# First mixer of a two-block network on one core: state space and attention interleaved pair by pair with 33 projection chunks

## The chip, the cores and the metric

The kernel runs on one core of a Trainium2 chip. The metric is device time in microseconds (us) of one execution of the whole program; lower is better. TensorE (PE) multiplies, VectorE (DVE) and ScalarE (ACT) do the elementwise work, GpSimd (POOL) does a few small things, and SyncE (SP) issues every DMA. Each engine runs its own list of instructions strictly in order and waits on semaphores for the others.

## The reference

The network has two blocks over 256 tokens of width 1024, all in float32. The change touches only the mixer of the first block, and none of its mathematics:

```python
def hybrid_mixer(h, ...):
    z, xbc, dt_raw, q, k, v, g_ssd, g_att = split_columns(h @ w_in)
    y_ssd = ssd_mixer(z, xbc, dt_raw, ...) @ w_ssd_out
    q, k = rope(q, positions), rope(k, positions)
    y_att = moba_attention(q, k, v) @ w_attn_out      # one block of 256 keys: causal softmax
    merged = sigmoid(g_ssd) * y_ssd + sigmoid(g_att) * y_att
    return merged @ w_out

def ssd_mixer(z, xbc, dt_raw, ...):                   # 16 heads of 64, 2 groups, state 64
    xs, Bm, Cm = split(silu(causal_dwconv(xbc, conv_w, conv_b)))
    dt = softplus(dt_raw + dt_bias); A_cum = cumsum(-dt * exp(a_log))
    y = (C B^T masked, times exp(A_cum[l] - A_cum[s])) @ (xs * dt) + xs * d_skip
    yg = (y * silu(z)) in 2 groups of 512 columns
    return yg * rsqrt(mean(yg * yg, last axis) + 1e-6) * norm_w
```

After the mixer come a mixture of experts, a gated embedding and a second block of four layers. They are the same in both kernels.

## The kernel before

**Chunks.** Every large weight is streamed in chunks of 1 MB (1024 rows by 256 columns) through three slots (`RING` = 3). SP loads chunk c into `raw` when chunk c-3's low part has been made. ACT copies it to `ring_hi`, rounded to fp32r (function `high`, called by `part`, L1716), when PE has used chunk c-3; DVE takes the rest into `ring_lo` (`low`, L2163). PE multiplies a chunk in 48 products of 256 columns, high by high, high by low and low by high (`product_f` L904, `product_t` L923), and DVE reads the result from PSUM ("drains" it; `drain`, L2187). `chunk_used` and `drained` count the chunks that PE has finished and that DVE has read.

**Stages.** The mixer runs as a sequence of stages: 9 + 8 + 4 + 8 chunks of the input projection (`in_zx`, `in_qk`, `in_v`, `in_g`), then the state space (`ssd`, a loop over pairs of heads, two pairs a round), 4 chunks of `ssd_out`, then attention (`attention`, the same kind of loop), 4 chunks of `attn_out`, `ple`, and 4 chunks of `mix_out`. No chunk is multiplied while `ssd` or `attention` runs. What sets the order on each engine is the order in which the code calls its pieces.

**One pair of heads in `ssd`.** PE spreads the summed decays over the partitions (L1020), DVE takes gaps from them (L2344), ACT takes exp (L1855), DVE weighs them with C B^T (L2351), PE multiplies with the weighted inputs (L1029, L1031), DVE adds the skip (L2357) and the gate (L2360). After the eight pairs, the norm of each group g of 512 columns goes: ACT squares (L1861), PE sums the squares over partitions and so leaves the sum in every partition (L1038), ACT takes the square root with scale and eps (L1865, which loads a table), DVE takes the reciprocal (L2365), multiplies (L2368) and splits into high and low parts (L2373, L2374) for `ssd_out`.

**One pair of heads in `attention`.** PE rotates q and k with a matrix (L1048), DVE combines with cosine and sine (L2418 to L2423), PE scores (L1058), DVE masks and takes the row maximum (L2388, L2393), ACT takes exp (L1771), DVE divides by the sum (L2401), PE transposes (L1075), ACT and DVE copy the halves (L1775, L2406), PE multiplies by the values (L1085, L1087), ACT and DVE split the result (L1778, L2410).

**POOL** computes 1/sqrt for the token norms as a power of -0.5 (`norm_root`, L1672, two columns) and, in the second block, powers of 16 columns (L1692), a product of 256 columns (L1675) and sums of 768 columns (L1703).

Of the kernel before, what the change touches and what calls it, by code (L numbers as in the profile page):

```python
# [26 lines left out]
P = 128  # L27
SEQ, D = 256, 1024
# [23 lines left out]
CREDIT = 1  # L52
# [4 lines left out]
STREAM = [("in_zx", 9), ("in_qk", 8), ("in_v", 4), ("in_g", 8), ("ssd_out", 4), ("attn_out", 4), ("ple", 1), ("mix_out", 4),  # L57
# [28 lines left out]
H_READY = [o for o in OPERANDS if o not in ("na", "hyena")]  # L86
# [230 lines left out]
def build(nc, A, out):  # L317
# [5 lines left out]
    with ctx:  # L323
# [48 lines left out]
        cum_diag = at("cum_diag", [HEADS, HEADS, SEQ], 71 * KB)  # L372
# [29 lines left out]
        sq_buf = at("sq_buf", [P, 4, SEQ], 71 * KB)  # L402
        ynorm = at("ynorm", [P, 4, SEQ], 75 * KB)
        rstd = at("rstd", [P, SEQ], 79 * KB)

        rope_t = at("rope_t", [P, 2, SEQ], 58 * KB)
        rope_u = at("rope_u", [P, 2, SEQ], 60 * KB)

        qk_st = [at(f"qk_st{u}", [P, 2, SEQ], (62, 87)[u] * KB) for u in range(2)]
        v_st = [at(f"v_st{u}", [P, TT, 2 * HD], (64, 89)[u] * KB) for u in range(2)]  # L410

        probs = [at(f"probs{u}", [P, 2, TT * SEQ], (65, 78)[u] * KB) for u in range(2)]
        probs_t = [at(f"probs_t{u}", [P, 2, TT * SEQ], (69, 82)[u] * KB) for u in range(2)]
        at_max = [at(f"at_max{u}", [P, 2, TT], 73 * KB + 96 * u) for u in range(2)]
        at_sum = [at(f"at_sum{u}", [P, 2, TT], 73 * KB + 96 * u + 32) for u in range(2)]
        at_inv = [at(f"at_inv{u}", [P, 2, TT], 73 * KB + 96 * u + 64) for u in range(2)]
# [89 lines left out]
        p_t = at("p_t", [P, TT, SEQ], 8 * KB)  # L506
        p_hi = at("p_hi", [P, 2, SEQ], 10 * KB, f32r)
        p_lo = at("p_lo", [P, 2, SEQ], 12 * KB, f32r)
# [43 lines left out]
        scores = [acc[:, 0:2, :], acc[:, 2:4, :]]  # L552
        turned_p = [[proj[:, 0, :], proj[:, 1, :]], [proj[:, 2, :], misc[:, :]]]
# [5 lines left out]
        def pair_of(bank):  # L559
# [34 lines left out]
        v_staged, p_turned, pt_act, pt_dve, o_ready, o_hi, o_read = (  # L594
            sem("v_staged"), sem("p_turned"), sem("pt_act"), sem("pt_dve"), sem("o_ready"), sem("o_hi"), sem("o_read"))
# [23 lines left out]
        xdt_ready, y_gated = sem("xdt_ready"), sem("y_gated")  # L619
# [33 lines left out]
        def unsorted_bank(q):  # L653

            return proj[:, q, :] if q < RING else misc[:, :]

# [41 lines left out]
        def _(sp):  # L698
# [84 lines left out]
            load_cols("in_zx", A["w_in"][0], 0, {0: load_params})  # L783
            for dst, src in ((tri[:, :, :], A["tri"].rearrange("p (t n) -> p t n", t=TT)), (diag16[:, :], A["diag16"]),
                             (dt_bias[:, :], A["dt_bias"][0].partition_broadcast(P)),
                             (a_log_b[:, :], A["a_log"][0].partition_broadcast(P)),
                             (w_dt[:, :, :], A["w_in"][0].rearrange("(k p) n -> p k n", p=P)[:, :, DT_COL:DT_COL + HEADS]),
                             (d_col[0:HD, :], A["d_skip"][0].rearrange("(i a) -> a i", a=2)[0].partition_broadcast(HD)),
                             (d_col[HD:P, :], A["d_skip"][0].rearrange("(i a) -> a i", a=2)[1].partition_broadcast(HD)),
                             (inv_freq[:, :], A["inv_freq"]), (rot[:, :], A["rot"]), (causal[:, :], A["causal"]),  # L790
                             (pos_i[:, :], A["positions"][0].partition_broadcast(P))):
                sp.dma_start(dst, src, allow_slow_non_contiguous=True).then_inc(mixer_tables, 16)
# [90 lines left out]
        def _(pe):  # L883
# [2220 lines left out]
```

## Time and profile before

| | us |
|---|---|
| median of 3 runs (2139.34 to 2152.94) | 2142.66 |
| the profiled execution's own time | 2141.7 |
| its span from the first to the last instruction | 2139.9 |
| mixer's first product to its last `attn_out` product | 19.89 to 384.7 |
| PE busy, share of the span | 93% |
| DVE busy | 65% |
| ACT busy | 43% |

The profiled execution is 0.96 us below the median. In the page's second part (40 slices of 53.5 us), PE stands at 9 tenths nearly everywhere, and falls to 5 to 8 tenths in slices 5 to 9, which are the mixer. In the same slices the row of the granted TensorE clock falls to 5 to 9 tenths, and the DMA row to nearly nothing in two of them.

### The profile page before, as it was taken

To read this page: it belongs to the slowest core of one execution; us is meant where nothing else is said; L and a number is where in the kernel's file an instruction comes from. 1 tells how busy PE (TensorE), PEld (TensorE's weight loads), DVE (VectorE), ACT (ScalarE), POOL (GpSimd) and SP (SyncE) were. 2 spreads that over 40 slices of the span, in tenths; PEclk is the share of its full clock that TensorE was granted. 3 is DMA by queue.
4 is the path that set the end of the run, shared out by engine and by line. 5 is a ranking of instruction groups with operands and counts; after the bars stand their busy time and mean duration, and the time that the engine had idled before them with its cause. 6 is when DMAs were issued, how large, how long until landed. Compare 5 with 4: busy or idle time off the path is not lost.

```text
span 2139.9 us, 33097 instructions
## 1 busy us (share of the span) xinstructions
PE 1982.1 (93%) x13478; PEld 1805.0 (84%) x13478; DVE 1396.8 (65%) x1579; ACT 917.5 (43%) x980; POOL 46.3 (2%) x65
## 2 busy tenths in 40 slices
PE   7999577889999997999999999998997999999999
PEld 6998365867777776999998999997887999999998
DVE  4566766576767766576666755557998555675665
ACT  4344233365656655343334543333434333434332
POOL 0000000000000000000101100000000000000000
PEclk9999587989999999999999999999999999999999
DMA  6644030167777774745554337554224555554553
GB/s 207 204 139 157 0 104 8 58 244 289 294 273 270 289 266 150 211 139 187 199 188 154 117 126 241 180 178 137 92 67 138 174 180 177 176 177 148 195 189 117
DMA packets 243909, 365.94 MB, mean 171 GB/s; under 512 B 12566, under 2 KB 217961, under 8 KB 231401
## 3 DMA queue, kind: packets, MB, share of 16 engines
q1 hardware_dynamic: 243817, 364.64, 50.4%
q8 instruction: 67, 1.10, 0.2%
q14 instruction: 25, 0.20, 0.0%
HBM read 363.57 MB, written 1.05 MB: 170 GB/s over the span
## 4 chain that ended last, share of the span: by engine, by line
PE 57%; DVE 12%; DMA 5%; ACT 4%; issue 3%; DVEq 0%; POOL 0%; ACTq 0%
PE proj L904 30%; PE acc L1098 10%; PE proj L923 7%; DMA raw<-in_w_exp_up_dram 5%; PE proj L1281 3%; DVE ring_lo L2163 2%; DVE ring_lo L2620 2%; PE acc L1251 2%; ACT ring_hi L1890 1%; ACT second_hi L1890 1%; ACT ring_hi L1716 1%; DVE second_lo L2620 1%; PE acc L1111 1%; PE acc L1357 1%; PE acc L948 1%
## 5 line engine op out<-in xcount | busy, mean ns | idle before, releaser
L2163 DVE TENSOR_TENSOR ring_lo<-raw,ring_hi 128x2048 fp32r<-128x2048 f32 x242 | 560.7, 2318 | 258.1 <-ACT ring_hi L1716 257.6
L1716 ACT ACTIVATE ring_hi<-raw 128x2048 fp32r<-128x2048 f32 x242 | 462.2, 1912 | 540.0 <-PE proj L904 300.3
L904 PE MATMUL proj<-h_hi,ring_hi 128*128 128x256 f32 x1936 | 558.3, 288 | 21.6 <-DVEq L2199 9.5
L904 PE MATMUL proj<-h_lo,ring_hi 128*128 128x256 f32 x1936 | 550.0, 284 | 0.0
L904 PE MATMUL proj<-h_hi,ring_lo 128*128 128x256 f32 x1936 | 549.9, 284 | 0.0
L904 PEld LDWEIGHTS proj<-h_hi,ring_hi 128*128 128x128 f32 x1936 | 372.9, 193 | 32.5 <-issue 21.8
L904 PEld LDWEIGHTS proj<-h_lo,ring_hi 128*128 128x128 f32 x1936 | 372.9, 193 | 2.5 <-issue 1.4
L904 PEld LDWEIGHTS proj<-h_hi,ring_lo 128*128 128x128 f32 x1936 | 372.6, 192 | 0.0
L904 PE MATMUL proj<-g_hi,ring_hi 128*128 128x256 f32 x704 | 196.4, 279 | 4.1 <-DVE hid L2470 4.1
L904 PE MATMUL proj<-g_lo,ring_hi 128*128 128x256 f32 x704 | 195.7, 278 | 0.0
L904 PE MATMUL proj<-g_hi,ring_lo 128*128 128x256 f32 x704 | 195.6, 278 | 0.0
L904 PEld LDWEIGHTS proj<-g_hi,ring_hi 128*128 128x128 f32 x704 | 133.0, 189 | 5.3 <-issue 4.5
L904 PEld LDWEIGHTS proj<-g_lo,ring_hi 128*128 128x128 f32 x704 | 133.2, 189 | 0.8
L904 PEld LDWEIGHTS proj<-g_hi,ring_lo 128*128 128x128 f32 x704 | 133.0, 189 | 0.0
L2620 DVE TENSOR_TENSOR second_lo<-raw,second_hi 128x2048 fp32r<-128x2048 f32 x48 | 109.9, 2292 | 32.4 <-ACT second_hi L1890 32.2
L2620 DVE TENSOR_TENSOR ring_lo<-raw,ring_hi 128x2048 fp32r<-128x2048 f32 x48 | 109.3, 2290 | 24.6 <-ACT ring_hi L1890 24.6
L1790 ACT ACTIVATE silu_g<-gate_in 128x512 f32<-128x512 f32 x44 | 27.8, 632 | 198.2 <-DVE gate_in L2461 198.2
L1890 ACT ACTIVATE second_hi<-raw 128x2048 fp32r<-128x2048 f32 x48 | 92.0, 1917 | 35.2 <-DMA raw<-in_w_exp_up_dram 16.9
L923 PE MATMUL proj<-ring_hi,h_hi 128*128 128x256 f32 x320 | 94.9, 297 | 9.2 <-DVE h_lo L2528 8.0
L1890 ACT ACTIVATE ring_hi<-raw 128x2048 fp32r<-128x2048 f32 x48 | 91.0, 1914 | 24.4 <-DMA raw<-in_w_exp_down_dram 9.4
L1098 PE MATMUL acc<-ring_hi,hid_lo 128*128 128x512 f32 x320 | 99.6, 393 | 0.0
L1098 PE MATMUL acc<-ring_lo,hid_hi 128*128 128x512 f32 x320 | 99.4, 392 | 0.0
(414 smaller groups left out, 3321.3 us busy)
## 6 DMA issues: line engine op xcount, KB each, us to landing
raw<-in_f_w_dram SPq DMA_DIRECT2D x132, 1024.0 KB, 5.0
raw<-in_w_exp_gate_dram SPq DMA_DIRECT2D x32, 1024.0 KB, 4.8
raw<-in_w_exp_up_dram SPq DMA_DIRECT2D x32, 1024.0 KB, 4.9
raw<-in_w_exp_down_dram SPq DMA_DIRECT2D x32, 1024.0 KB, 4.8
raw<-in_w_in_dram SPq DMA_DIRECT2D x29, 1024.0 KB, 5.2
raw<-in_a_w_in_dram SPq DMA_DIRECT2D x24, 1024.0 KB, 5.2
raw<-in_b_w_qkv_dram SPq DMA_DIRECT2D x12, 1024.0 KB, 5.1
raw<-in_c_w_in_dram SPq DMA_DIRECT2D x12, 1024.0 KB, 5.2
```

What stands on the lines that cost most here:

```text
L904: last = pe.matmul(bank[:, a, :], w[:, k, a * P:(a + 1) * P], h[:, k, :], start=(k == 0 and w is hi and h is h_h and (a == 0 or not first) ...
L923: last = pe.matmul(bank[:, t, :], h[:, k, t * P:(t + 1) * P], w[:, k, :], start=(k == 0 and w is hi and h is h_h), stop=(k == KT - 1 and h ...
L948: last = pe.transpose(turn_bank(operand, kk)[:, a, t * P:(t + 1) * P], x[:, t, k * P:(k + 1) * P], ident[:, :])
L1098: last = pe.matmul(acc[:, 2 * t + m, :], h[:, k, t * P:(t + 1) * P], w[:, k, m * HALF:(m + 1) * HALF], start=(start and k == 0 and h is hi ...
L1111: last = pe.matmul(acc[:, 2 * t + m, :], h[:, k, t * P:(t + 1) * P], w[:, k, m * HALF:(m + 1) * HALF], start=False, stop=(k == 1 and h is ...
L1251: last = pe.matmul(bank, h[:, k, 0:P], w[:, k, m * HALF:(m + 1) * HALF], start=(first and k == 0 and h is hid_hi and w is hi), stop=(k == ...
L1281: last = pe.matmul(pair(v % RING), h, w, start=(k == 0 and h is h_h and w is hi), stop=(k == KT - 1 and h is h_l))
L1716: act.activation(w_hi[n.slot][:, :], raw[n.slot][:, :], ACT.Copy).then_inc(hi_ready, 1)
L1790: act.activation(silu_g[:, :], gate_in[:, :, :].rearrange("p a n -> p (a n)"), ACT.Silu).then_inc(silu_ready, 1)
L1890: act.activation(dst, raw[c.slot][:, :], ACT.Copy).then_inc(hi_ready, 1)
L2163: dve.tensor_tensor(w_lo[n.slot][:, :], raw[n.slot][:, :], w_hi[n.slot][:, :].bitcast(f32), SUB)\
L2620: dve.tensor_tensor(dst, raw[c.slot][:, :], hi.bitcast(f32), SUB).then_inc(lo_ready, 1)
```

## The change

The mixer's stages become one list of 33 chunks (`MIXER`): x0 to x4 (state space inputs), z0 to z3, then q and k in turn, v, g (gate of the state space), a (gate of attention), s (`ssd_out`). Each kind of chunk has its own way of being drained, on two PSUM banks in turn (`mx_bank`); the third bank of `proj` takes the rotations. The pieces of the state space and of attention are cut into functions for one pair, and the code calls them between quarters of chunks: `project_mx(28, {1: ...})` runs the given calls after the first quarter (12 products) of chunk 28. ACT and DVE get matching lists of calls. `ssd_out` and `attn_out` get operands of their own (`ssd_hi`, `ssd_lo`, `attn_hi`, `attn_lo`), so attention no longer waits for `ssd_out` to release `h_hi` and `h_lo`.

Operations fall away or change: the `cum_diag` product (4096 columns) is replaced by a broadcast row of `diag16` as a weight; time steps are multiplied as 24 fp32r products with 16 weight columns (before, 32 products in float32 with 128 weight columns); the copies of values and of rotated q and k fall away; the rotation takes two tiles in one product; loops are unrolled. In the norm of a group, ACT now writes mean plus eps (Identity), **POOL** takes the power -0.5 of all 256 columns, and DVE multiplies in place; ACT makes the high part and DVE the low part. The mixer's tables are loaded after chunk 2 (before, after chunk 8).

```diff
+MIXER = ("x0 x1 x2 x3 x4 z0 z1 z2 z3 q0 k0 q1 k1 q2 k2 q3 k3 v0 v1 v2 v3 g0 g1 g2 g3 a0 a1 a2 a3 s0 s1 s2 s3").split()
+        def mx_bank(c):
+            return pair(c % 2)
...
+            def project_mx(c, between={}):
+                s, kind = Chunk(c), MIXER[c][0]
+                wait_parts(s)
+                if c > 1:
+                    pe.wait_ge(drained, c - 1)
+                product = product_t if kind == "v" else product_f
+                product(s, "ssd" if kind == "s" else "attn", MIXER[c] in ("x0", "s0"), between, mx_bank(c))
...
-                for g in range(SSD_GROUPS):
-                    pe.wait_ge(y_squared, g + 1)
-                    for a in range(4):
-                        last = pe.matmul(acc[:, g, 0:SEQ], ones[:, :], sq_buf[:, a, :], start=(a == 0), stop=(a == 3))
-                    last.then_inc(y_ssq, 1)
+            def sum_squares(g):
+                pe.wait_ge(decays_made, 2)
+                pe.wait_ge(y_squared, 3 * g + 1)
+                for a in range(4):
+                    last = pe.matmul(misc[:, 0:SEQ], ones[:, :], sq_buf[:, a, :], start=(a == 0), stop=(a == 3))
+                last.then_inc(y_ssq, 1)
+            def score_pair(i):
+                pe.wait_ge(roped, 2 * (i // 2) + 2)
+                if i:
+                    pe.wait_ge(masked, i)
...
+            def mixer():
...
+                project_mx(25)
+                spread_sums(7)
+                mix_states(5)
+                sum_squares(0)
+                mix_states(6)
+                score_pair(0)
+                project_mx(26, {1: lambda: mix_states(7), 3: lambda: score_pair(1)})
+                project_mx(27, {3: lambda: (turn_pair(0), score_pair(2))})
+                sum_squares(1)
+                project_mx(28,
+                           {1: lambda: (values_of_pair(0), turn_pair(1), score_pair(3), rotate_chunk(7)),
+                            3: lambda: (turn_pair(2), score_pair(4))})
...
             norm_root("attn")
+            for g in range(SSD_GROUPS):
+                pool.wait_ge(y_squared, 3 * g + 2)
+                if g:
+                    pool.wait_ge(y_normed, 2 * g - 1)
+                pool.tensor_tensor(rstd[:, :], mean_f[:, :], neg_half[:, 0:1].to_broadcast([P, SEQ]), POW).then_inc(y_root, 1)
...
-                act.activation(rstd[:, :], acc[:, g, 0:SEQ], ACT.Sqrt, bias=eps_col[:, 0:1],
-                               scale=1.0 / (SSD_INNER // SSD_GROUPS)).then_inc(y_root, 1)
+            def mean_group(g):
+                act.wait_ge(y_ssq, g + 1)
+                if g:
+                    act.wait_ge(y_root, g)
+                act.activation(mean_f[:, :], misc[:, 0:SEQ], ACT.Identity, bias=eps_col[:, 0:1],
+                               scale=1.0 / (SSD_INNER // SSD_GROUPS)).then_inc(y_squared, 1)
+            def high_group(g):
+                act.wait_ge(y_normed, 2 * g + 1)
...
+            part(Chunk(25))
+            mean_group(0)
+            decays(7)
+            high_group(0)
+            exp_pair(0)
...
-                link(dve.reciprocal(rstd[:, :], rstd[:, :]))
+            def norm_group(g):
+                dve.wait_ge(y_gated, 4 * g + 4)
                 dve.wait_ge(y_root, g + 1)
+                for a in range(4 * g, 4 * g + 4):
+                    col = ROW["ssd_norm_w"] + a
+                    last = dve.scalar_tensor_tensor(out=pj[:, a, :], in0=pj[:, a, :], scalar=params[:, col:col + 1], in1=rstd[:, :],
                                                     op0=MUL, op1=MUL)
                 last.then_inc(y_normed, 1)
+            def low_group(g):
+                dve.wait_ge(y_squared, 3 * g + 3)
+                tiles = slice(4 * g, 4 * g + 4)
+                dve.tensor_tensor(ssd_lo[:, tiles, :], pj[:, tiles, :], ssd_hi[:, tiles, :].bitcast(f32), SUB).then_inc(y_normed, 1)
```

What stands on POOL between the token norms. Before, the norm of the first block's input is followed at once by the next token norm (the rows are the last two of one norm, the diagonal for its spreading, and the next norm):

```order
L1671 TENSOR_SCALAR ms<-ms 128x2
L1672 TENSOR_TENSOR inv<-ms,neg_half 128x2
L1675 TENSOR_TENSOR inv_diag<-ident_sb,inv 128x256
L1670 TENSOR_TENSOR ms<-ssq 128x2
L1671 TENSOR_SCALAR ms<-ms 128x2
L1672 TENSOR_TENSOR inv<-ms,neg_half 128x2
```

In the change two operations of 256 columns stand between them:

```order
L1827 TENSOR_SCALAR ms<-ms 128x2
L1828 TENSOR_TENSOR inv<-ms,neg_half 128x2
L1831 TENSOR_TENSOR inv_diag<-ident_sb,inv 128x256
L1845 TENSOR_TENSOR rstd<-mean_f,neg_half 128x256 x2
L1826 TENSOR_TENSOR ms<-ssq 128x2
L1827 TENSOR_SCALAR ms<-ms 128x2
L1828 TENSOR_TENSOR inv<-ms,neg_half 128x2
```

L1845 is the power -0.5 of a group's means, L1828 that of the token norm.

DVE at the norm of the first group. Before, it stands behind all pairs of the state space, in a block with the second group's, with attention far behind:

```order
L2360 TENSOR_TENSOR pj<-pj,y_sum 128x256
L2331 REGISTER_ALU
L2331 COMPARE_AND_BRANCH
L2365 RECIPROCAL rstd<-rstd 128x256
L2368 SCALAR_TENSOR_TENSOR ynorm<-pj,params,rstd 128x256 x4
L2373 CAST h_hi<-ynorm 128x1024
L2374 TENSOR_TENSOR h_lo<-ynorm,h_hi 128x1024
L2365 RECIPROCAL rstd<-rstd 128x256
L2368 SCALAR_TENSOR_TENSOR ynorm<-pj,params,rstd 128x256 x4
```

In the change it stands between the drain of chunk 25 (L2554) and the first rows of attention; L2692 is `norm_group(0)`, L2715 the mask of pair 0, L2436 the low part of chunk 27:

```order
L2554 TENSOR_TENSOR pj<-proj,inv_b 128x512
L2647 TENSOR_TENSOR xdt_72<-xs_t,dt_t 128x256
L2684 TENSOR_TENSOR pj<-pj,y_sum 128x256
L2669 TENSOR_TENSOR decay_w_70<-decay_w_70,cb 128x768
L2692 SCALAR_TENSOR_TENSOR pj<-pj,params,rstd 128x256 x4
L2715 SCALAR_TENSOR_TENSOR probs_102<-acc,causal_sb 128x768
L2677 SCALAR_TENSOR_TENSOR y_sum<-conv,d_col,acc 128x256
L2724 TENSOR_REDUCE at_max_106<-probs_102 128x2 x2
L2436 TENSOR_TENSOR ring_lo<-raw,ring_hi 128x2048
```

The norm moved from the end of a stage into the middle of DVE's list, and everything behind it there, weights' low parts and attention alike, waits with it.

DVE at the norm of the second group, in the change (before, it is the second `RECIPROCAL` row above). L2700 is `low_group(0)`, L2746 a copy of transposed scores, L2735 the division of pair 2, the second L2692 row kind is `norm_group(1)`, L2715 the mask of pair 3:

```order
L2700 TENSOR_TENSOR ssd_lo<-pj,ssd_hi 128x1024
L2746 COPY probs_t_105<-acc 128x384
L2732 RECIPROCAL at_inv_110<-at_sum_108 128x4
L2735 TENSOR_SCALAR probs_102<-probs_102,at_inv_110 128x128
L2735 TENSOR_SCALAR probs_102<-probs_102,at_inv_110 128x256
L2735 TENSOR_SCALAR probs_102<-probs_102,at_inv_110 128x128
L2735 TENSOR_SCALAR probs_102<-probs_102,at_inv_110 128x256
L2692 SCALAR_TENSOR_TENSOR pj<-pj,params,rstd 128x256 x4
L2715 SCALAR_TENSOR_TENSOR probs_103<-acc,causal_sb 128x768
```

It stands inside attention's pairs, with pairs 3 to 7 and the chunks 29 to 32 behind it.

## Rows read from the trace of the kernel before

**Rows 1.** Windows by stage: stretch, its length, busy time (instructions) of PE, PEld, DVE, ACT, POOL; granted clock, DMA share, GB/s.

```profile
19.90:203.70 183.80, 183.72 (x1468) 182.57 (x1468) 109.33 (x111) 66.30 (x49) 0.00 (x0) 0.97 0.55 176
203.70:265.50 61.80, 34.71 (x137) 23.66 (x137) 46.56 (x90) 22.88 (x20) 0.00 (x0) 0.63 0.05 16
265.50:291.70 26.20, 25.46 (x192) 25.26 (x192) 9.64 (x7) 6.44 (x4) 0.00 (x0) 0.90 0.44 138
291.70:361.00 69.30, 38.97 (x209) 26.40 (x209) 50.83 (x105) 31.11 (x93) 0.00 (x0) 0.70 0.08 28
361.00:385.40 24.40, 24.40 (x200) 24.26 (x201) 15.40 (x17) 6.92 (x5) 0.00 (x0) 1.00 0.37 102
```

**Rows 2.** Timeline of DVE: start, length, instruction; drains of chunks 1 and 16, last merge.

```profile
34.25 0.69 DVE L2187 TENSOR_TENSOR pj<-proj,inv_b 128x512 f32<-128x512 f32 x1 [1.94 <-PE proj L904]
...
120.65 0.69 DVE L2187 TENSOR_TENSOR pj<-proj,inv_b 128x512 f32<-128x512 f32 x1 [1.52 <-PE proj L904]
...
384.71 0.69 DVE L2430 TENSOR_TENSOR merge_t<-proj,pj 128x512 f32<-128x512 f32 x1 [0.35 <-PE proj L904]
```

**Rows 3.** Timeline of PE: short products of the two loops, x = records merged.

```profile
204.50 1.51 PE L1004 MATMUL proj<-ident_sb,conv 128*128 128x128 f32 x12 [0.88 <-DVE pj L2187]
...
239.17 2.29 PE L1020 MATMUL acc<-cum_diag,ones 16*128 x8
...
255.25 1.99 PE L1038 MATMUL acc<-sq_buf,ones 128*128 128x256 f32 x8 [1.51 <-ACT sq_buf L1861]
...
308.10 0.66 PE L1085 MATMUL acc<-probs_t,v_st 128*64 128x256 f32 x4
308.58 0.40 PE L1087 MATMUL acc<-probs_t,v_st 128*64 128x128 f32 x4
308.87 0.66 PE L1085 MATMUL acc<-probs_t,v_st 128*64 128x256 f32 x4
309.32 0.42 PE L1087 MATMUL acc<-probs_t,v_st 128*64 128x128 f32 x4
309.68 1.99 PE L1048 MATMUL proj<-pj,rot_sb 128*128 x8
```

**Rows 4.** Groups by line on POOL, whole span: busy us, mean ns, idle before.

```profile
L1703 POOL TENSOR_TENSOR na_bias<-na_runs,na_mask_sb 128x768 f32<-128x768 f32 x8 | 13.6, 1705 | 130.8 <-DVE hid_lo L2478 130.8
L1692 POOL TENSOR_TENSOR rate<-rate_in,neg_half 128x16 f32<-128x16 f32 x4 | 11.6, 2900 | 59.5 <-DVE rate_in L2758 59.5
L1672 POOL TENSOR_TENSOR inv<-ms,neg_half 128x2 f32<-128x2 f32 x12 | 8.3, 695 | 1.0
L1675 POOL TENSOR_TENSOR inv_diag<-ident_sb,inv 128x256 f32<-128x256 f32 x9 | 5.5, 613 | 0.7
```

**Rows 5.** Timeline of POOL and DVE where a POOL sum and a low part meet.

```profile
1052.43 1.69 POOL L1703 TENSOR_TENSOR na_bias<-na_runs,na_mask_sb 128x768 f32<-128x768 f32 x1 [14.67 <-DVE hid_lo L2478]
1053.23 3.05 DVE L2163 TENSOR_TENSOR ring_lo<-raw,ring_hi 128x2048 fp32r<-128x2048 f32 x1 [0.88 <-ACT ring_hi L1716]
```

**Rows 6.** Groups by line from 0 to 420 us: weight parts, and root and reciprocal.

```profile
L2163 DVE TENSOR_TENSOR ring_lo<-raw,ring_hi 128x2048 fp32r<-128x2048 f32 x42 | 96.0, 2290 | 39.2 <-ACT ring_hi L1716 39.0
...
L2365 DVE RECIPROCAL rstd<-rstd 128x256 f32<-128x256 f32 x2 | 3.5, 1754 | 5.4 <-ACT rstd L1865 5.4
...
L1865 ACT ACT_TABLE_LOAD x1 | 1.3, 1283 | 0.0
L1865 ACT ACTIVATE rstd<-acc,eps_col 128x256 f32<-128x256 f32 x2 | 0.9, 473 | 5.1 <-DVE ynorm L2368 2.7 <-PE acc L1038 2.4
```

**Rows 7.** Windows as in rows 1: one round (two pairs) of `ssd`, one of attention's softmax.

```profile
222.68:231.50 8.82, 6.38 (x25) 4.20 (x24) 7.09 (x16) 2.97 (x3) 0.00 (x0) 0.50 0.00 0
315.40:327.30 11.90, 7.96 (x42) 5.80 (x43) 8.12 (x21) 6.12 (x21) 0.00 (x0) 0.59 0.00 0
```

**Rows 8.** Windows after PE's wait of 8.25 us at 265.5.

```profile
265.50:270.50 5.00, 5.00 (x23) 5.00 (x24) 0.00 (x0) 0.00 (x0) 0.00 (x0) 0.50 0.00 0
270.50:275.50 5.00, 5.00 (x44) 5.00 (x43) 0.69 (x1) 1.78 (x1) 0.00 (x0) 1.00 0.00 0
```

**Rows 9.** Windows in a mixer of the second block that is already interleaved with chunks.

```profile
1600.00:1650.00 50.00, 38.08 (x286) 36.16 (x285) 42.29 (x65) 16.65 (x18) 0.00 (x0) 0.93 0.37 121
```

More of the change, by code:

```diff
@@ L84 @@
             "ffn1", "mix2", "hyena", "ffn2", "mix3", "conv1", "ffn3"]
-H_READY = [o for o in OPERANDS if o not in ("na", "hyena")]
+H_READY = [o for o in OPERANDS if o not in ("ssd", "attention", "na", "hyena")]
 CONVS = ((0, 0), (1, 0), (0, 1), (2, 0), (1, 1), (3, 0), (2, 1), (3, 1))
@@ new lines, in _ @@
+            drain_mx(20)
+            weigh_xs(0)
+            keep_sums()
+            weigh_xs(1)
+            gaps(0)
+            gaps(1)
+            mask_states()
+            weigh_decays(0)
+            part(Chunk(21))
+            drain_mx(21)
+            roped_tiles(5)
+            weigh_decays(1)
+            weigh_xs(2)
+            gaps(2)
+            add_skip(0)
+            part(Chunk(22))
+            weigh_decays(2)
+            drain_mx(22)
+            gate_y(0)
+            drain_mx(23)
@@ new lines, in _ @@
+            weigh_xs(3)
+            gaps(3)
+            add_skip(1)
+            gaps(4)
+            gate_y(1)
+            weigh_xs(4)
+            add_skip(2)
+            weigh_decays(3)
+            weigh_decays(4)
+            gate_y(2)
+            weigh_xs(5)
+            gaps(5)
+            add_skip(3)
+            gate_y(3)
+            add_skip(4)
+            weigh_decays(5)
+            gaps(6)
+            weigh_xs(6)
+            part(Chunk(23))
+            drain_mx(24)
+            weigh_decays(6)
@@ new lines, in _ @@
+            gate_y(4)
+            gaps(7)
+            add_skip(5)
+            drain_mx(25)
+            weigh_xs(7)
+            gate_y(5)
+            weigh_decays(7)
+            norm_group(0)
+            masked_rows(0)
+            add_skip(6)
+            row_max(0)
+            part(Chunk(24))
+            gate_y(6)
+            masked_rows(1)
+            drain_mx(26)
+            add_skip(7)
+            norm_rows(0)
+            row_max(1)
+            gate_y(7)
+            part(Chunk(25))
@@ new lines, in _ @@
+            masked_rows(2)
+            row_max(2)
+            keep_turned(0)
+            roped_tiles(6)
+            norm_rows(1)
+            low_group(0)
+            keep_turned(1)
+            norm_rows(2)
+            norm_group(1)
+            masked_rows(3)
+            row_max(3)
+            drain_mx(27)
+            low_of_pair(0)
+            part(Chunk(26))
+            masked_rows(4)
+            norm_rows(3)
+            keep_turned(2)
+            low_group(1)
+            drain_mx(28)
```

961 lines of the change are left out of this document (623 added, 338 removed).

## The prediction

> **What bounds the kernel now.** I began with the busy shares: TensorE (PE) is busy 93% of the span, so elsewhere only less PE work would help. The exception is the mixer, and the windows by stage show it [rows 1]. The projections are full (183.72 busy of 183.80 us, granted clock 0.97). Then come two stages in which PE holds 34.71 of 61.8 and 38.97 of 69.3 us, at granted clocks of 0.63 and 0.70, that is partly at 1.2 GHz instead of 2.4. DVE isn't full there either (46.56 and 50.83 us): a round of two pairs takes 8.82 us in `ssd`, with 7.09 of DVE, and 11.90 us in attention, with 8.12 of DVE and a clock of 0.50 to 0.59 [rows 7]. These 131 us are a chain in which PE, DVE and ACT wait for one another. Chunks of weights between the pairs would fill PE's gaps and raise its clock; a mixer of the second block built so has a clock of 0.93 and PE busy 38.08 of 50 us [rows 9]. What can be had is PE's idle time plus what the low clock costs, about half of 131 us and a little more.
>
> **What the change puts in the way.** The norm of a group was an ACT root of 0.47 us and a DVE reciprocal of 1.75 us, and one table load of 1.28 us [rows 6]. Now POOL takes a power of 128x256, twice. No such operation of this width is in the trace, but there are two narrow ones [rows 4]: 2 columns take 695 ns, 16 columns 2900 ns. That is (2900 - 695) / 14 = 157.5 ns a column and 0.38 us beside, so 0.38 + 256 x 0.1575 = **40.7 us** for one power. The bounds: 2900 / 16 = 181 ns a column gives 46.4 us, 695 / 2 = 347 ns gives 88.8 us; from below, a POOL product of 256 columns takes 0.61 us [rows 4]. I take 40.7, since two rows of the same operation lie behind it, and the 16 columns are the nearest in width.
>
> A sum on POOL goes at 1705 / 768 = 2.2 ns a column [rows 4], seventy times cheaper than the power. The Trainium skill (GPSIMD Engine Reference, section 3.1, Elementwise) gives GpSimd's two-input operation about 2.6 cycles an element, from an add of 2048 columns in 4497 ns. By it, as an estimate, the power would take 0.6 us. The sum's row agrees with that page, the two power rows don't; this case comes back as the first rival.
>
> The order shows who pays. `norm_group(0)` stands in the middle of DVE's list, between chunk 25's drain and attention's first mask, and `norm_group(1)` between pairs 2 and 3 of attention. DVE reaches the first some 2 us after the power can start, and the second some 4 us after. So about 36 us of each power are an idle DVE, and behind DVE stand low parts (2.29 us each [rows 6]), drains and attention. PE soon runs out: at quarter 1 or 3 of chunk 26, and within chunk 28. The powers do not lie beside other work.
>
> **A lock during the power.** In the trace POOL's sum ran from 1052.43 to 1054.12, and a low part issued at 1053.23 ended at 1056.28, having lasted 3.05 us [rows 5] instead of 2.29 [rows 6]. It lasted 0.76 us longer and ended 2.16 us after POOL, as if it had begun when POOL was done. The Trainium skill (SBUF — State Buffer, section "SBUF: two separate sides") calls the shared ports an exclusive lock held for a whole instruction, against DVE operations with two SBUF inputs; by that rule, the trace agrees. So I assume that DVE's `weigh_xs(7)`, `gate_y(5)` and `weigh_decays(7)`, and at the second power `low_group(0)`, also wait for POOL's end. Their work, 1.8 us and 1.3 us, and what hangs on it then comes after the powers. No row shows this with a power: without it the sum is some 6 us shorter.
>
> **The walk, leg by leg**, in us from the span's start. Chunks run at (120.65 - 34.25) / 15 = 5.76 each [rows 2], so one product of 256 columns is 0.12 and a quarter 1.44.
>
> A, up to the end of chunk 20: chunk 1 is drained at 34.25, and 19 more chunks give 143.7. Between them stand six rotations of about 0.85 (eight records of L1048 take 1.99 [rows 3] at a lower clock), 24 products for the time steps (2.9), and transposes (0.7): 8.7 in all. End: **152.4**. DVE's own list up to here is about 72 us of work, with room.
>
> B, to the start of the first power: chunks 21 to 25, 28.8. PE's work for a pair is 6.38 / 2 = 3.19 at a clock of 0.50 [rows 7], so 1.6 at full clock, about half each for spread and mix: eight spreads (6.8) and six mixes (4.8). Squares of the group 2.0 (L1038 [rows 3]), C B^T, transposes and the first score 4.1 (twelve records of L1004 take 1.51 [rows 3]), the mean 0.5 (like the root). That is 47.0; DVE has about as much work in this stretch, so I add 4 for handoffs: 51, to **203.4**.
>
> C, first power: 40.7, to **244.1**.
>
> D, to the start of the second: the locked DVE work 1.8, mix 7 0.8, two quarters at the low clock 5.1, score 1.7, a quarter 1.4, chunk 27 with a turn and a score 7.2, squares 2.0, mean 0.5: 20.5, with 3.5 for handoffs 24, to **268.1**.
>
> E, second power: 40.7, to **308.8**.
>
> F, to `attn_out`'s last merge: DVE has from `low_group(0)` to the last split of attention about 46.7 of work (five pairs at 8.12 / 2 = 4.06 [rows 7], six low parts 13.7, drains, norm and splits the rest), 51 with its waits. Then 3.5 chunks of 5.76 (20.2), a turn (0.6; the products of a pair lie between 308.10 and 309.7 [rows 3]), 2.4 for a clock that is low at first (after PE's wait, 5 us brought 23 products at a clock of 0.50, the next 5 us 44 at 1.00 [rows 8]), and 3 for handoffs: 77, to **385.8**.
>
> The last merge is at 384.71 before [rows 2]; so the mixer ends 1.1 us later. What follows it is the same. The earlier loads of the mixer's tables cost nothing: SP queues them for a slot or two of the ring, and chunks wait for low parts, not for SP (the transfers' share is 0.55 in that stretch [rows 1]). If that cover were gone, it would be about 8 us. 2141.7 + 1.1 = 2142.8 for the profiled execution, which lies 0.96 below the median; I predict **2143**. In words: the interleaving gains about 80 us, and the two powers cost that much again. The forecast's own range follows from the price (46.4 each adds 11.4), the lock (-6) and the handoffs (about 10 either way): 2127 to 2160.
>
> **Rivals.** One per cent, about what a measurement of this kernel can tell from no change, is 2121 to 2164.
>
> *The power costs what a POOL product costs.* Then legs C and E shrink from 81.4 to about 2, DVE never waits, D and F lose the recovery of the clock, and `attn_out` ends near 302: about **2058**. For it: L1675 and L1703; against it: both rows of the very operation. The GPSIMD page of the Trainium skill, named above, is on this side. 0.11.
>
> *The price per column falls with width.* At 100 to 120 ns a column a power is 26 to 31 us and the sum gives **2113 to 2124**. For it: the step from 2 to 16 columns already lowers the mean price from 347 to 181 ns; against it: a constant 0.38 us explains that. 0.09.
>
> *PE's clock stays low, and the kernel is slower.* PE idles some 37 us twice, and behind each power it gets its work in pieces. In the two stages of before that look so, the granted clock was 0.63 and 0.70 [rows 1]. Legs D and F hold about 76 us of PE work; at 0.70 they take 76 / 0.70 - 76 = 33 more, less some 6 that hide beside DVE: **2170**. It decides from a clock below about 0.8 between the powers and behind the second. Against it: after 8.25 us of idleness the clock was back at 1.00 after 5 us [rows 8], and the interleaved mixer holds 0.93 [rows 9]. 0.10.
>
> **How the numbers follow.** The linear price with a recovering clock gets 0.70, the rivals 0.11, 0.09 and 0.10. The predicted time is that of the first. The range must leave out no more than 2 in 10: I leave out 2058, and reach down to 2108, for the price that falls with width, and up to 2168, for most of the slow clock. Faster by over 1% are the cheap power and most of the falling price, 0.19 with a little of the forecast's lower end: 0.20. Slower by over 1%: the slow clock, with a little from the upper end, 0.11. The rest is 0.69.
>
> **What would show it.** On POOL, two powers at L1845 of about 41 us each: that decides nearly everything. DVE idle for some 36 us ahead of both L2692 groups, ended by POOL; PE idle about as long in chunks 26 and 28. The pace of 5.76 up to chunk 20 at about 152, the first power's start at about 203, the second's at 268, the last merge at about 386. That DVE operations with two SBUF inputs end right behind a power would show the lock. The prediction falls with a power of a few us, with granted clocks below 0.8 behind the powers, or if DVE, not PE, already paces chunks 9 to 20.

## The result, and the profile after

| | before | after |
|---|---|---|
| median of 20 runs, us | 2145.11 | 2132.63 |
| ratio after / before | | 0.994, 95% interval 0.993 to 0.995 |
| span of the profiled execution | 2139.9 | 2127.1 |
| last merge of `attn_out` in it | 384.71 [rows 2] | 370.52 |

The change is 0.6% faster, about 12.5 us. That is within the one per cent named ahead, but it is a clear gain where the forecast was 2143 us and no gain. The trace holds the same difference in the mixer alone: the last merge comes 14.19 us sooner, and what follows it takes about as long as before (2139.9 - 384.71 = 1755.2 us, and 2127.1 - 370.52 = 1756.6).

POOL of the kernel after, groups by line over the whole span (busy, mean ns, idle before), and then its two powers in the timeline (start, length):

```profile
L1845 POOL TENSOR_TENSOR rstd<-mean_f,neg_half 128x256 f32<-128x256 f32 x2 | 83.8, 41876 | 210.0 <-ACT mean_f L2017 210.0
L1851 POOL TENSOR_TENSOR rate<-rate_in,neg_half 128x16 f32<-128x16 f32 x4 | 11.6, 2899 | 59.5 <-DVE rate_in L3256 59.5
L1828 POOL TENSOR_TENSOR inv<-ms,neg_half 128x2 f32<-128x2 f32 x12 | 8.3, 695 | 1.0
```

```profile
203.53 41.32 POOL L1845 TENSOR_TENSOR rstd<-mean_f,neg_half 128x256 f32<-128x256 f32 x1 [193.02 <-ACT mean_f L2017]
261.86 42.43 POOL L1845 TENSOR_TENSOR rstd<-mean_f,neg_half 128x256 f32<-128x256 f32 x1 [17.00 <-ACT mean_f L2017]
```

Who waits for them, in the waits of DVE and PE between 200 and 310 us (us in total, times, longest):

```profile
DVE pj L2692 <- POOL rstd L1845: 77.8, 2, 39.5
PE acc L1128 <- DVE probs L2715: 74.9, 2, 37.5
```

These two rows hold nearly all the waiting of the stretch: DVE stands for 77.8 us at the norms, and PE stands for 74.9 us behind DVE, at the scores of a pair, since DVE has not yet masked the scores before them. In the windows by leg (columns as in [rows 1]) it looks like this:

```profile
19.90:158.20 138.30, 137.06 (x1098) 133.13 (x1099) 91.22 (x113) 55.97 (x50) 0.00 (x0) 0.99 0.55 178
158.20:203.53 45.33, 45.12 (x325) 37.28 (x323) 36.80 (x75) 21.72 (x20) 0.00 (x0) 1.00 0.29 95
203.53:210.20 6.67, 6.58 (x57) 5.46 (x52) 1.92 (x4) 0.66 (x1) 6.67 (x1) 1.00 0.01 2
210.20:244.90 34.70, 0.00 (x0) 0.00 (x0) 0.00 (x0) 0.00 (x0) 34.66 (x1) 0.56 0.00 0
244.90:261.86 16.96, 14.22 (x97) 12.89 (x98) 16.62 (x32) 10.77 (x23) 0.00 (x0) 0.79 0.36 120
261.86:270.00 8.14, 7.89 (x62) 6.24 (x60) 3.10 (x9) 6.41 (x13) 8.14 (x1) 1.00 0.03 10
270.00:304.30 34.30, 0.00 (x0) 0.00 (x0) 0.00 (x0) 0.00 (x0) 34.29 (x1) 0.53 0.00 0
304.30:351.20 46.90, 44.12 (x354) 39.28 (x355) 40.99 (x72) 25.89 (x61) 0.00 (x0) 0.90 0.42 141
351.20:371.00 19.80, 19.80 (x169) 19.68 (x168) 17.30 (x18) 8.02 (x6) 0.00 (x0) 1.00 0.61 176
```

Up to the first power PE is busy in 137.06 of 138.30 and 45.12 of 45.33 us at full clock: the interleaving does what it says. Then PE works 6.58 us beside the first power, and 34.70 us pass with nothing but POOL. The same happens in the second, with 7.89 us of PE's work beside it and 34.30 us of nothing. The change took PE's idle time and low clock in the two loops away [rows 1] and put 69 us of standstill in.

### The profile page after: what moved, and what is told of

Read it like the earlier page. It is cut to its first block, busy times and chain, and to the rows that moved or that the text cites. A ratio compares the mean times of both kernels' runs of the same rounds, so it can differ in the third digit from the quotient of the medians.

```text
span 2127.1 us, 32529 instructions
## 1 busy us (share of the span) xinstructions
PE 1952.0 (92%) x13424; PEld 1779.0 (84%) x13424; DVE 1372.9 (65%) x1567; ACT 914.5 (43%) x984; POOL 130.0 (6%) x67
## 4 chain that ended last, share of the span: by engine, by line
PE 58%; DVE 12%; DMA 5%; ACT 4%; issue 3%; DVEq 0%; POOL 0%; ACTq 0%
PE proj L932 30%; PE acc L1271 10%; PE proj L951 7%; DMA raw<-in_w_exp_up_dram 5%; PE proj L1454 3%; DVE ring_lo L3118 2%; DVE ring_lo L2436 2%; ACT ring_hi L2163 1%; PE acc L1424 1%; ACT second_hi L2163 1%; DVE second_lo L3118 1%; ACT ring_hi L1875 1%; PE acc L1530 1%; PE acc L1284 1%; PE acc L976 1%
## 5 line engine op out<-in xcount | busy, mean ns | idle before, releaser
L2436 DVE TENSOR_TENSOR ring_lo<-raw,ring_hi 128x2048 fp32r<-128x2048 f32 x242 | 560.2, 2317 | 234.7 <-ACT ring_hi L1875 234.1
L932 PE MATMUL proj<-h_hi,ring_hi 128*128 128x256 f32 x1808 | 524.7, 290 | 13.0 <-DVE ring_lo L2436 8.4
L932 PE MATMUL proj<-h_lo,ring_hi 128*128 128x256 f32 x1808 | 513.6, 284 | 0.0
L932 PE MATMUL proj<-h_hi,ring_lo 128*128 128x256 f32 x1808 | 513.4, 284 | 0.0
L932 PEld LDWEIGHTS proj<-h_hi,ring_hi 128*128 128x128 f32 x1808 | 347.9, 192 | 27.5 <-issue 15.5
L932 PEld LDWEIGHTS proj<-h_lo,ring_hi 128*128 128x128 f32 x1808 | 348.0, 192 | 3.5 <-issue 2.4
L932 PEld LDWEIGHTS proj<-h_hi,ring_lo 128*128 128x128 f32 x1808 | 347.8, 192 | 0.0
```

What stands on the lines that cost most here:

```text
L932: last = pe.matmul(bank[:, a, :], w[:, k, a * P:(a + 1) * P], h[:, k, :], start=(k == 0 and w is hi and h is h_h and (a == 0 or not first) ...
L2436: dve.tensor_tensor(w_lo[n.slot][:, :], raw[n.slot][:, :], w_hi[n.slot][:, :].bitcast(f32), SUB)\
```

## The experiments

In all of them a ratio is to the kernel before in runs on the same chip, and a median alone is to be read beside its ratio: the median of before was 2145.11, 2147.91 and 2150.31 in the three sets.

### The powers taken out

```diff
-            for g in range(SSD_GROUPS):
-                pool.wait_ge(y_squared, 3 * g + 2)
...
-                pool.tensor_tensor(rstd[:, :], mean_f[:, :], neg_half[:, 0:1].to_broadcast([P, SEQ]), POW).then_inc(y_root, 1)
...
-                act.activation(mean_f[:, :], misc[:, 0:SEQ], ACT.Identity, bias=eps_col[:, 0:1],
+                act.activation(mean_f[:, :], misc[:, 0:SEQ], ACT.Sqrt, bias=eps_col[:, 0:1],
...
             def norm_group(g):
+                dve.wait_ge(y_squared, 3 * g + 2)
+                dve.reciprocal(rstd[:, :], mean_f[:, :]).then_inc(y_root, 1)
```

> The change as it is, but the norm of each group goes by a root on ACT and a reciprocal on DVE again, without the POOL power. Theory (the two powers are on the path nearly whole, and the interleaving itself is worth some 90 us): DVE's waits ahead of the norms, 39.47 and 38.35 us in the changed kernel, vanish; two reciprocals of 1.75 us and a table load or two come in; 2132.6 - 77.8 + 4 to 8 gives 2059 to 2063, the last merge of attn_out at about 296 to 302. Rival (DVE and PE wait for one another in this stretch anyway, so that other waits take the powers' place): under 50 us less, above 2080.

Measured: 2061.34 us, ratio 0.9586 (0.9558 to 0.9613). From 0.994 to 0.9586 is 3.5%, some 76 us: nearly all of the 77.8 us that DVE waited. The norms in DVE's timeline (start, length, idle before in brackets where there is any) with the last merge, the two roots on ACT, and the window from 20 to 290 us:

```profile
206.26 1.75 DVE L2685 RECIPROCAL rstd<-mean_f 128x256 f32<-128x256 f32 x1
208.04 1.67 DVE L2689 SCALAR_TENSOR_TENSOR pj<-pj,params,rstd 128x256 f32<-128x256 f32 x4
228.83 1.74 DVE L2685 RECIPROCAL rstd<-mean_f 128x256 f32<-128x256 f32 x1
295.95 0.69 DVE L2925 TENSOR_TENSOR merge_t<-proj,pj 128x512 f32<-128x512 f32 x1 [0.49 <-PE proj L932]
```

```profile
202.72 0.47 ACT L2012 ACTIVATE mean_f<-misc,eps_col 128x256 f32<-128x256 f32 x1 [0.58 <-PE misc L1106]
223.63 0.47 ACT L2012 ACTIVATE mean_f<-misc,eps_col 128x256 f32<-128x256 f32 x1 [1.14 <-PE misc L1106]
```

```profile
20.00:290.00 270.00, 265.22 (x2096) 244.92 (x2097) 205.35 (x312) 131.78 (x173) 0.00 (x0) 1.00 0.46 145
```

DVE reaches both norms without waiting; the last merge stands at 295.95, where 296 to 302 was expected. PE is busy 98% of the mixer at full clock, DVE 76%. The rival, that other waits would take the powers' place, falls.

### The price of a power

```diff
-                pool.tensor_tensor(rstd[:, :], mean_f[:, :], neg_half[:, 0:1].to_broadcast([P, SEQ]), POW).then_inc(y_root, 1)
+                pool.memset(rstd[:, 64:SEQ], 1.0)
+                pool.tensor_tensor(rstd[:, 0:64], mean_f[:, 0:64], neg_half[:, 0:1].to_broadcast([P, 64]), POW).then_inc(y_root, 1)
```

> The POOL power takes only the first 64 of the 256 columns; the other 192 columns of the root are set to 1, so most tokens are not normed. Theory (a price per column): from 41.3 us for 256 columns and 0.70 for 2 a column costs 0.16 us, so each power lasts 10.6 us, DVE's two waits fall by 31 us each, and the time is 2132.6 - 62 = 2071. Rival (the price has a large fixed part, or falls with width): a power of 64 columns lasts over 14 us.

Measured: 2068.84 us, ratio 0.9625 (0.9598 to 0.9651). POOL's group of the power, and DVE's two norms with their waits and the last merge:

```profile
L1846 POOL TENSOR_TENSOR rstd<-mean_f,neg_half 128x64 f32<-128x64 f32 x2 | 21.1, 10543 | 0.0
```

```profile
215.86 1.67 DVE L2693 SCALAR_TENSOR_TENSOR pj<-pj,params,rstd 128x256 f32<-128x256 f32 x4 [9.18 <-POOL rstd L1846]
243.34 1.67 DVE L2693 SCALAR_TENSOR_TENSOR pj<-pj,params,rstd 128x256 f32<-128x256 f32 x4 [6.78 <-POOL rstd L1846]
...
308.16 0.69 DVE L2929 TENSOR_TENSOR merge_t<-proj,pj 128x512 f32<-128x512 f32 x1 [0.44 <-PE proj L932]
```

Four widths now lie on one line: 2 columns 0.695, 16 columns 2.90, 64 columns 10.54 and 256 columns 41.3 to 42.4 us. From 64 to 256 a column costs (41.32 - 10.54) / 192 = 0.160 us, and 0.3 us stand beside. The waits fell by 30.3 and 31.6 us, and the last merge comes 62.4 us sooner (308.16 for 370.52): what a power is shortened by comes back whole. The time, 3.15% below the change by the ratios (some 68 us, with intervals of about 6 us either way), goes with it.

### What runs beside a power

```diff
+            dve.wait_ge(y_gated, 4)
+            for _ in range(16):
+                link(dve.tensor_tensor(ssd_hi[:, 0:4, :], pj[:, 0:4, :], pj[:, 0:4, :], SUB))
             norm_group(0)
```

> Sixteen extra differences of 1024 columns with two SBUF inputs, whose result nobody reads, stand on DVE ahead of the first norm_group, at the start of the first power. If the power leaves DVE its ports, each takes about 1.25 us (the 1024-column difference of low_group took 1.23), all 20 us lie within the wait of 39.5 us, and the time stays at 2133. If the ports are locked as in the meeting of a POOL sum and a low part, the first ends with the power, and the time grows by about 19 us to 2152.

Measured: 2137.48 us, ratio 0.9935 (0.9898 to 0.9971), that of the change. DVE's timeline:

```profile
205.30 0.72 DVE L2684 TENSOR_TENSOR pj<-pj,y_sum 128x256 f32<-128x256 f32 x1
205.94 0.94 DVE L2669 TENSOR_TENSOR decay_w<-decay_w,cb 128x768 f32<-128x768 f32 x1
206.81 20.11 DVE L2861 TENSOR_TENSOR ssd_hi<-pj 128x1024 fp32r<-128x1024 f32 x16
246.39 1.67 DVE L2692 SCALAR_TENSOR_TENSOR pj<-pj,params,rstd 128x256 f32<-128x256 f32 x4 [19.47 <-POOL rstd L1845]
```

Sixteen differences in 20.11 us, each at its ordinary length, and the wait is shorter by just that (19.47 instead of 39.47). So the power doesn't make such operations wait for its end. Only the gate (L2684), which begins 0.36 us after the power, took 0.72 us here and in the change, where it took 0.42 in the run without powers. To see whether that lies in the power or in this place, eighteen POOL sums took the place of the first power:

```diff
...
+                if g == 0:
+                    for n in range(18):
+                        pool.tensor_tensor(scratch[:, :, :], pj[:, 0:4, :], pj[:, 0:4, :], ADD).then_inc(small, 1)
+                        pool.wait_ge(small, n + 4)
+                    pool.memset(rstd[:, :], 1.0).then_inc(y_root, 1)
+                    continue
...
             weigh_decays(7)
+            dve.wait_ge(y_gated, 4)
+            for _ in range(16):
+                link(dve.tensor_tensor(ssd_hi[:, 0:4, :], pj[:, 0:4, :], pj[:, 0:4, :], SUB))
             norm_group(0)
```

> The run with sixteen extra differences on DVE, but with eighteen POOL sums of 1024 columns (two SBUF inputs, 2.2 ns a column, about 2.25 us each, 41 us in all) in place of the first power; the first group's root is set to 1, so that group is not normed. If a POOL sum locks DVE out for its length and the power does not, the differences last some 3.4 us instead of 1.26, or as many sums are lengthened by them, and both together take about 60 us instead of lying side by side: sums and differences end only after about 41 + 20 us, and the time is some 15 to 20 us above 2137. If DVE and POOL run side by side, the differences stay at 1.26 us and the time at 2137.

Measured: 2142.38 us, ratio 0.9973 (0.995 to 0.9995). The timelines of POOL and DVE:

```profile
203.28 49.16 POOL L1848 TENSOR_TENSOR scratch<-pj 128x1024 f32<-128x1024 f32 x18 [192.59 <-ACT mean_f L2024]
```

```profile
203.65 2.00 DVE L2691 TENSOR_TENSOR pj<-pj,y_sum 128x256 f32<-128x256 f32 x1
205.57 2.65 DVE L2676 TENSOR_TENSOR decay_w<-decay_w,cb 128x768 f32<-128x768 f32 x1
208.14 45.38 DVE L2868 TENSOR_TENSOR ssd_hi<-pj 128x1024 fp32r<-128x1024 f32 x16
253.56 1.67 DVE L2699 SCALAR_TENSOR_TENSOR pj<-pj,params,rstd 128x256 f32<-128x256 f32 x4
```

The same sixteen differences take 45.38 us, the gate (L2691) 2.00 instead of 0.42 and `weigh_decays` (L2676) 2.65 instead of 0.95. So POOL's sums do hold DVE up here, and the power, of the same engine, does not. Single instructions out of the two rows of x18 and x16, the first, third and fourth sum, then the first two differences:

```profile
203.28 2.08 POOL L1848 TENSOR_TENSOR scratch<-pj 128x1024 f32<-128x1024 f32 x1 [192.59 <-ACT mean_f L2024]
207.48 2.49 POOL L1848 TENSOR_TENSOR scratch<-pj 128x1024 f32<-128x1024 f32 x1
210.04 2.75 POOL L1848 TENSOR_TENSOR scratch<-pj 128x1024 f32<-128x1024 f32 x1
208.14 2.91 DVE L2868 TENSOR_TENSOR ssd_hi<-pj 128x1024 fp32r<-128x1024 f32 x1
211.08 2.80 DVE L2868 TENSOR_TENSOR ssd_hi<-pj 128x1024 fp32r<-128x1024 f32 x1
```

The two take turns: a sum ends at 209.97, a difference at 211.05, the next sum at 212.79, the next difference at 213.88. One sum and one difference go through in 2.83 us, and sixteen such turns make some 45 us. That both read `pj` is not the reason, since `weigh_decays` reads other tiles and was held up as well. Only the size was not as expected: 20 us and some 41 us would have made 60, and the two were through after 50 us (203.28 to 253.5). The 60 us added whole lengths, with a sum taken at 2.25 us from the rows of 768 columns. The first sum, while the gate stood behind it, took 2.08 us, and within a turn the difference needs 1.1 us from the sum's end and the sum 1.7 us from the difference's end. Against the run with the power the norm came 7.2 us later. The time is 0.4% up (some 8 us), less than the 15 to 20 us put down; the two intervals overlap, so the time alone would not show it.

### The powers put elsewhere

Each group's mean got a buffer of its own (in place, `roots[g]`), and both norms moved back in DVE's list:

```diff
...
             weigh_decays(7)
-            norm_group(0)
             masked_rows(0)
...
             norm_rows(2)
-            norm_group(1)
             masked_rows(3)
...
             row_max(4)
+            norm_group(0)
+            low_group(0)
+            norm_group(1)
+            low_group(1)
             masked_rows(5)
```

> The change with the same two POOL powers, but with a buffer for each group's mean, and with both groups' norms and splits moved back in DVE's list, behind the first rows of pair 4, just ahead of where chunk 29 needs them (ACT's high parts move along). Theory (what costs is DVE's in-order wait, so the place counts as much as the price): the second power follows the first at once and ends at about 288 instead of 304.3, and some 13 us of DVE's later work is done by then: 371 becomes about 340, 30 us less than the change, 2102. Rival (a power costs its length wherever it stands): 2125 to 2135.

Measured: 2111.85 us, ratio 0.9821 (0.9791 to 0.9852): 1.2% below the change, some 25 us, and 5 to 10 us short of what was expected. The norms in DVE's timeline, the last merge, and the window behind the second power:

```profile
246.81 1.94 DVE L2689 SCALAR_TENSOR_TENSOR pj<-pj,params,mean_f 128x256 f32<-128x256 f32 x4 [6.90 <-POOL mean_f L1844]
287.88 1.67 DVE L2689 SCALAR_TENSOR_TENSOR pj<-pj,params,rstd 128x256 f32<-128x256 f32 x4 [36.79 <-POOL rstd L1844]
347.39 0.69 DVE L2925 TENSOR_TENSOR merge_t<-proj,pj 128x512 f32<-128x512 f32 x1 [0.49 <-PE proj L933]
```

```profile
287.80:347.40 59.60, 55.45 (x453) 52.13 (x454) 46.89 (x73) 31.14 (x57) 0.00 (x0) 0.92 0.43 133
```

The first wait fell from 39.47 to 6.90 us, since DVE now has the first pairs' rows to do meanwhile; the second stayed, for by then nothing else was left that could go ahead of it. The second power ended at 287.8, as expected, 16.5 us sooner than in the change; behind it 59.6 us were needed, not 53. Against the windows of the change from 304.30 to 371.0, DVE has 46.89 us of work in this leg instead of 58.3 and PE 55.45 instead of 63.9, and the leg is about 7 us shorter. A likely reading, not tried by itself, is that what DVE was spared counts only as far as PE was spared work too. The rival (a power costs its length wherever it stands) falls: each power is as long as before, and the last merge comes 23.1 us sooner. The run moves the norms and lets the second power follow the first at once, and it doesn't part the two.

### The power alone in the kernel before

```diff
...
-                act.activation(rstd[:, :], acc[:, g, 0:SEQ], ACT.Sqrt, bias=eps_col[:, 0:1],
+                act.activation(rstd[:, :], acc[:, g, 0:SEQ], ACT.Identity, bias=eps_col[:, 0:1],
...
+            for g in range(SSD_GROUPS):
+                pool.wait_ge(y_root, g + 1)
+                pool.tensor_tensor(rstd[:, :], rstd[:, :], neg_half[:, 0:1].to_broadcast([P, SEQ]), POW).then_inc(y_pow, 1)
...
-                dve.wait_ge(y_root, g + 1)
-                link(dve.reciprocal(rstd[:, :], rstd[:, :]))
+                dve.wait_ge(y_pow, g + 1)
```

> The kernel before with one part of the change alone: the POOL power of 256 columns in place of root and reciprocal, in place on the same buffer. Theory: each group's norm grows by a power of 41.9 us and loses the reciprocal (1.75) and a table load (1.28), so 2145 + 2 x 38.9 = 2223. Rival (the second group's power lies beside the first group's split and the first chunk of ssd_out): some 10 us less, 2210 to 2214.

Measured: 2221.85 us, ratio 1.0346 (1.0311 to 1.0381), that is 3.1 to 3.8% over the kernel before. DVE's timeline:

```profile
290.28 1.67 DVE L2371 SCALAR_TENSOR_TENSOR ynorm<-pj,params,rstd 128x256 f32<-128x256 f32 x4 [44.97 <-POOL rstd L1690]
333.85 1.67 DVE L2371 SCALAR_TENSOR_TENSOR ynorm<-pj,params,rstd 128x256 f32<-128x256 f32 x4 [39.55 <-POOL rstd L1690]
457.66 0.69 DVE L2433 TENSOR_TENSOR merge_t<-proj,pj 128x512 f32<-128x512 f32 x1 [0.35 <-PE proj L905]
```

The last merge is at 457.66, 72.95 us behind that of before: some 5 us less than the sum of 78. Of these, 1.6 us are the powers, which took 41.13 and 41.12 us instead of the 41.9 put down, and 2.3 us the first group's split (0.69 and 1.57 us), which now lies beside ACT's step and the second power. The interval holds both the sum and the upper part of the rival's range, so the time alone doesn't tell them apart. With the run without powers, the two parts of the change are now measured singly: the powers alone cost 3.5%, the rest alone brings 4.1%, and the difference is the 0.6%.

### A version without powers and reciprocals

```diff
-            for g in range(SSD_GROUPS):
-                pool.wait_ge(y_squared, 3 * g + 2)
...
-                pool.tensor_tensor(rstd[:, :], mean_f[:, :], neg_half[:, 0:1].to_broadcast([P, SEQ]), POW).then_inc(y_root, 1)
...
                 act.wait_ge(y_ssq, g + 1)
+                act.activation(mean_f[:, :], misc[:, 0:SEQ], ACT.Ln, bias=eps_col[:, 0:1],
+                               scale=1.0 / (SSD_INNER // SSD_GROUPS)).then_inc(y_squared, 1)
+                act.wait_ge(y_squared, 3 * g + 2)
                 if g:
-                    act.wait_ge(y_root, g)
-                act.activation(mean_f[:, :], misc[:, 0:SEQ], ACT.Identity, bias=eps_col[:, 0:1],
-                               scale=1.0 / (SSD_INNER // SSD_GROUPS)).then_inc(y_squared, 1)
+                    act.wait_ge(y_normed, 2 * g - 1)
+                act.activation(rstd[:, :], mean_f[:, :], ACT.Exp, scale=-0.5).then_inc(y_root, 1)
```

> As the run with root and reciprocal, but ACT makes the root alone: logarithm of the mean, then exp of -0.5 times it; no reciprocal on DVE (3.5 us less there). If PE is the bound of the stretch once the powers are gone (it was busy 265.22 of the 270 us from 20 to 290 with the root back), the time hardly moves: 2057 to 2062, at most 5 us below 2061. If DVE is the bound, at least 3.5 us fall out of the time, and the last merge moves from 295.95 to 292.

Measured: 2059.60 us, ratio 0.9579 (0.9554 to 0.9605). The last merge and the window from 20 to 290 us:

```profile
293.81 0.69 DVE L2925 TENSOR_TENSOR merge_t<-proj,pj 128x512 f32<-128x512 f32 x1 [0.49 <-PE proj L932]
```

```profile
20.00:290.00 270.00, 266.89 (x2115) 246.75 (x2116) 204.07 (x315) 134.91 (x177) 0.00 (x0) 1.00 0.47 147
```

It differs from the run with root and reciprocal (0.9586) by less than either interval; in the trace the merge comes 2.1 us sooner, less than the 3.5 us of DVE's work left out. PE, at 266.89 of 270 us, is what bounds the mixer now. Both versions beat the kernel before by about 4% and the change by about 3.5%.

## Why the prediction was right, and where it was wrong

**The main mechanism was right.** The powers took 41.32 and 42.43 us where 40.7 was put down, so the linear price from the rows of 2 and 16 columns [rows 4] held over a sixteenfold step, and each power was an idle DVE nearly whole (39.47 and 38.35 us; 36 was put down). By the rule of about 2.6 cycles an element for GpSimd (the Trainium skill, GPSIMD Engine Reference, section 3.1, Elementwise) a power would have been, as an estimate, 0.6 us. The rows of 2, 16, 64 and 256 columns all stand against carrying that figure from an add to a power. The first two rivals, a cheap power and a price that falls with width, go with them.

**The legs up to the first power came out right, the second of them in part by luck.** PE ended chunk 20 at 152.85 (152.4 predicted); the first power began at 203.53 (203.4). Leg B counted 47 us of work and 4 us for handoffs, which no row stood for. The window of that leg shows PE without gaps:

```profile
152.85:203.53 50.68, 50.47 (x370) 42.63 (x368) 41.91 (x84) 26.19 (x25) 0.00 (x0) 1.00 0.32 105
```

So PE had some 50 us of work there and next to no handoffs, and the two errors cancelled.

**The step that failed is the size of legs D and F**, both too long, and with them the sign. From the end of the first power to the start of the second, leg D, it took 17.0 us instead of 24 (244.85 to 261.86), and from the end of the second to the last merge, leg F, 66.2 instead of 77 (304.29 to 370.52). The powers were 2.35 us longer together than taken, and the first began 0.1 us later. 385.8 - 7.0 - 10.8 + 2.4 + 0.1 makes 370.5, the merge that the trace has. That is 15.3 us less than the sum had, and the median of 2132.63 lies 10.4 us below 2143; the profiled execution, of 2128.9 us, is 3.7 us faster than that median.

*Leg D: the lock.* The prediction carried over from [rows 5] that DVE operations with two SBUF inputs wait for POOL's end, so that `weigh_decays(7)`, the mix behind it and two quarters of chunk 26 came after the power. In the change DVE did all three operations right at the power's start (at 203.53):

```profile
203.45 0.42 DVE L2647 TENSOR_TENSOR xdt<-xs_t,dt_t 128x256 f32<-128x256 f32 x1
203.90 0.72 DVE L2684 TENSOR_TENSOR pj<-pj,y_sum 128x256 f32<-128x256 f32 x1
204.54 0.95 DVE L2669 TENSOR_TENSOR decay_w<-decay_w,cb 128x768 f32<-128x768 f32 x1
```

PE did mix 7 and the two quarters within 6.58 us beside it. That was 7.7 us of the leg (1.8 + 0.8 + 5.1). The run without powers has this work undivided: from the end of the first group's root on ACT to the end of the second's (203.19 to 224.10) it took 20.9 us at full clock, where the leg's 24 hold some 2 us for a low clock. So the work was sized about rightly and put on the wrong side of the power. The runs with sixteen differences show the cause directly: 20.11 us beside a power, 45.38 us beside sums. The trace disagrees with the section "SBUF: two separate sides" of the Trainium skill's page SBUF — State Buffer for the power. It agrees with it for the sums, which took turns with the differences. The prediction had said that no row showed the lock with a power, and that without it the sum was some 6 us shorter; with that value it would have forecast 2137. The 6 were too few: by the terms here the lock carried 7.7 us in leg D and 3.1 in leg F.

*Leg F: surcharges that overlap.* Three parts. First, 3.10 us of DVE's work (`low_group(0)` among it) ran beside the second power, again without a lock. Second, DVE's work up to attention's last split was 40.99 us behind the power, 44.1 with those 3.10, where 46.7 was counted, 2.6 too many; the waits in it were 5.9 instead of 4.3. Third, 6 us were added at the end for a low clock, handoffs and a turn (2.4 + 3 + 0.6), and none of it came there (0.9 us more was saved since PE had 32 of `attn_out`'s 192 products behind it at the last split, where half a chunk, 24, was counted): from 351.2 to 371.0 PE was busy in 19.80 of 19.80 us at full clock. The clock was low behind the second power, as put down, but there DVE set the pace. The windows behind it:

```profile
307.00:312.00 5.00, 4.92 (x23) 4.30 (x24) 5.00 (x7) 2.40 (x10) 0.00 (x0) 0.50 0.00 0
312.00:317.00 5.00, 5.00 (x39) 4.37 (x39) 4.96 (x9) 0.00 (x0) 0.00 (x0) 0.87 0.61 210
317.00:322.00 5.00, 5.00 (x46) 4.57 (x46) 4.96 (x13) 4.18 (x11) 0.00 (x0) 1.00 0.64 213
```

DVE is busy 5.00 of 5.00 us while PE runs at 1.2 GHz: both delays were in the sum one after the other, and they lie side by side. That the low clock cost nothing is read from these rows and was not tried by itself.

**The third rival**, a clock that stays low, did not come true, though its mark was just touched: over the whole leg the granted clock was 0.79 between the powers, where the prediction had named 0.8, and 0.90 behind the second. It did not stay low. Between the powers it rose in steps:

```profile
244.90:250.00 5.10, 2.36 (x11) 1.74 (x12) 5.04 (x9) 2.22 (x6) 0.00 (x0) 0.50 0.00 0
250.00:255.00 5.00, 5.00 (x37) 5.00 (x36) 4.96 (x12) 4.95 (x7) 0.00 (x0) 0.81 0.57 191
255.00:261.86 6.86, 6.86 (x53) 6.15 (x52) 6.61 (x13) 3.60 (x12) 0.00 (x0) 1.00 0.46 158
```

Behind the second it was 1.00 from 317 on, and both legs came out shorter than forecast, not longer.

**What was predicted of the gain was right in kind**: "the interleaving gains about 80 us, and the two powers cost that much again". The runs put it at 4.1% (about 88 us) and 3.5% (about 74 us). The forecast was the difference of two large terms, so errors of 7 and 11 us in legs of 24 and 77 decided the sign.

## What to carry to other kernels

Price an operation by the same operation in other widths, never by another operation of its engine: two rows, of 2 and 16 columns, gave 41 us where the engine's sums, at 2.2 ns a column [rows 4], would have given 0.6. Here a slow operation on an idle engine cost nearly its whole length, because an engine waited for it in the middle of an in-order list; look at who waits and what is queued behind, and make the value on an engine that is quick at it, or wait as late as its reader allows. Where a forecast is the difference of two large terms, give the surcharges (handoffs, clocks, contention) to one engine's path only, and ask of each which other delay it lies beside.

## What the runs showed of the hardware

POOL's power costs 0.16 us a column from 2 to 256 columns (41.1 to 42.4 us at 256 columns, over all these runs). DVE operations with two SBUF inputs ran beside it at a pace of 1.26 us each, their ordinary length; the one that met its start took 0.72 us instead of 0.42. POOL's sums of 1024 columns and the same DVE operations took turns, one of each in 2.83 us. What decides it, the way the power reads its operands or something else, was not tried.
